# First layer: where the key searches of query blocks 4 to 7 run, and the order in which the blocks are attended

## What is computed

```python
logits = jnp.einsum('bqhd,bsd->bqhs', qi, k_idx)
score = jnp.einsum('bqh,bqhs->bqs', wi, jax.nn.relu(logits))
score = jnp.where(causal[None], score, -jnp.inf)
_, idx = lax.top_k(score, topk)            # topk = 256
c_sel = jax.vmap(lambda c, i: c[i])(c_kv, idx)
s = jnp.einsum('bqhr,bqkr->bhqk', qa, c_sel)
p = jax.nn.softmax(jnp.where(valid[:, None], s, -jnp.inf), axis=-1)
```

## Time and profile before

| | us |
|---|---|
| median of three runs | 4326.2 |
| span of the profiled execution | 4323.5 |
| second half of stage 1, last input tile turned to last projection | 457 to 800 |
| stage 2, recurrence and attention of layer one | 827 to 2172 |

### The profile page before, as it was taken

How to read it: one execution, slowest core, us unless ns; L and a number is a source line. 1 busy time by engine, 2 the same in 40 slices (tenths; PEclk the granted TensorE clock), 3 DMA queues, 4 the chain that set the end, 5 groups by cost and what they waited for, 6 DMA issues and landing times. The chain is left out here.

```text
span 4323.5 us, 76198 instructions
## 1 busy us (share of the span) xinstructions
PE 3949.5 (91%) x31096; PEld 2780.8 (64%) x31096; DVE 2669.1 (62%) x5092; ACT 2122.4 (49%) x3127; POOL 1204.6 (28%) x966
## 2 busy tenths in 40 slices
PE   7989999878988998888789899898999999999889
PEld 5767776546666666666477687686555555555567
DVE  5555555556777787788675323345677777777543
ACT  4444444397777888787443322222333333333431
POOL 1111111125344344434111000000444445454200
PEclk9999999887999999999789999999999999999999
DMA  3334233402111111211255544465232323231243
GB/s 124 95 115 131 83 99 102 124 20 50 34 42 39 47 44 37 56 44 48 86 181 186 197 138 147 167 217 175 52 77 54 80 61 77 55 81 34 99 141 107
DMA packets 388093, 404.95 MB, mean 94 GB/s; under 512 B 115776, under 2 KB 287488, under 8 KB 387488
## 3 DMA queue, kind: packets, MB, share of 16 engines
q1 hardware_dynamic: 386656, 396.77, 31.3%
q10 hardware_dynamic: 1088, 3.32, 0.2%
HBM read 248.36 MB, written 151.62 MB: 93 GB/s over the span
## 5 line engine op out<-in xcount | busy, mean ns | idle before, releaser
L142 ACT ACTIVATE PT<-psum 128x1024 f32<-128x1024 f32 x384 | 394.3, 1027 | 659.6 <-PE psum L132 659.1
L170 DVE TENSOR_REDUCE m<-psum 128x1 f32<-128x1024 f32 x384 | 467.9, 1221 | 274.8 <-PE psum L132 274.8
L132 PE MATMUL psum<-xc,wah 128*128 128x512 f32 x1600 | 514.8, 403 | 3.2 <-DVE xc L146 2.9
L146 POOL TENSOR_TENSOR part<-PT 128x1024 f32<-128x1024 f32 x144 | 341.5, 2371 | 471.4 <-DVE all L146 379.1
L132 PE MATMUL psum<-PT,V 128*64 128x512 f32 x1536 | 371.5, 605 | 0.0
L143 ACT ACTIVATE bias<-score,cand,cols 128x2048 bf16<-128x2048 f32 (+6 forms) x217 | 314.8, 1451 | 85.9 <-DVE cand L153 79.5
L146 POOL TENSOR_TENSOR Lm<-gm,cst 64x512 f32<-64x512 f32 x192 | 257.6, 1342 | 349.9 <-PE psum L132 194.2
L132 PEld LDWEIGHTS psum<-xc,wah 128*128 128x128 f32 x1600 | 300.0, 190 | 79.4 <-issue 10.3
L143 ACT ACTIVATE sgn<-score,cand,cols 128x1920 bf16<-128x1920 f32 (+6 forms) x217 | 291.4, 1343 | 89.5 <-DVE cand L153 84.8
L132 PE MATMUL psum<-hc,w4h 128*128 128x512 f32 x1024 | 320.3, 394 | 8.7 <-DVE w4l L146 8.7
L132 PE MATMUL psum<-xc,wal 128*128 128x512 f32 x800 | 315.9, 395 | 0.0
(11 more groups left out here) (336 smaller groups left out, 8664.9 us busy)
## 6 DMA issues: line engine op xcount, KB each, us to landing
raw_a<-in_w_a SPq DMA_DIRECT2D x50, 512.0 KB
raw_w<-in_w_in SPq DMA_DIRECT2D x32, 512.0 KB, 5.3
QNh<-scr_qnh SPq DMA_DIRECT2D x48, 256.0 KB, 4.9
QRh<-scr_qrh SPq DMA_DIRECT2D x96, 128.0 KB, 4.6
QNl<-scr_qnl SPq DMA_DIRECT2D x48, 256.0 KB, 6.4
xin<-in_x SPq DMA_DIRECT2D x16, 512.0 KB
scr_AR<-AR SPq DMA_DIRECT2D x32, 256.0 KB, 2.2
scr_BK<-BK SPq DMA_DIRECT2D x32, 256.0 KB, 2.2
```

The source lines that it names most:

```text
L132: return self.e.matmul(out, a, b, start=start, stop=stop, skip_group_check=True)
L142: return self.e.activation(out, src, f, bias=bias, scale=scale)
L146: return self.e.tensor_tensor(out, a, b, op) if self.e else self.vector(out)
L170: return self.e.tensor_reduce(out, a, AX, op, negate=negate) if self.e else self.vector(a)
```

## The change

The searches of blocks 7, 6, 5 and 4 move from stage 2 into stage 1, after the last input tile is turned. The search code becomes one set of functions (`index_pe`, `index_act`, `index_dve`, `index_pool`) that both stages call with their own buffers (class `Search`). In stage 1 the searches take freed buffers: the two input tiles for the scores, the scratch of the transposes for the keys and signs, and PSUM banks 4 and 5, which DVE reads directly after an in-place relu. Each finished bias is stored to DRAM, and stage 2 loads the four at its start. The blocks are then attended in the order 7, 6, 5, 4, 15, ..., 8, 3, 2, 1, 0; block 7 follows the keys and values in their round, blocks 6 to 4 have the next. The number of passes per search is the same.

```diff
+N_EARLY = 4
+BLOCKS = (7, 6, 5, 4, 15, 14, 13, 12, 11, 10, 9, 8, 3, 2, 1, 0)
...
+        early.score = xin
+        early.kidx, early.keys_there = [xtmp[1].rearrange("p a b -> p (a b)"), ekidx], (d_eki, 1)
+        signs = [xjunk, xtmp[0].bitcast(BF16).rearrange("p a b -> p (a b)")]
+        early.junk = early.out = lambda b: signs[early.lane(b)]
+        early.relu = lambda k, e: bank[4 + e]
+        order_e = []
+        for t in early.blocks + [N_EARLY]:
+            halves_e = ([index_half(t - 1, True)] if t else []) + ([index_half(t, False)] if t < N_EARLY else [])
+            order_e += weave(weight, *halves_e)
...
         order_a += carry_a
+        ready = order_a.index(("tr", NT - 1)) + 1
+        order_a = order_a[:ready] + merge(order_a[ready:], order_e)
...
+                elif k[0] == "qx":
+                    b = k[1]
+                    if early.no[b] == 0:
+                        q.wait_ge(n_act, "xh", NT - 1, 1)
+                        q.wait_ge(n_dve, "xl", NT - 1, 1)
+                        q.wait_ge(d_kv[1], 1)
+                        for c in range(2):
+                            q.dma(early.kidx[c][:, :], scratch["kidx"][:, 512 * c:512 * c + 512]).then_inc(*d_eki.up(c))
...
+                    q.dma(eqx[:, :, :], feat("q")[:, 4:6, 128 * nth(b):128 * nth(b) + 128]).then_inc(*d_eqx.up(b))
+                elif k[0] == "tie" and k[2] == last_of[k[1]]:
+                    b, n = k[1:]
+                    N = 128 * (nth(b) + 1)
+                    q.wait_ge(early.k_pool, "tie", b, n)
+                    q.dma(scratch["bias"][early.no[b]][:, 0:N], early.out(b)[:, 0:N]).then_inc(*d_ebo[early.lane(b)].up(b))
...
-        for t in range(-1, NT + 1):
-            parts = [attend_pieces((t - 1,))] if t > 0 else [kv_order] if t < 0 else []
-            parts += [index_half(t, True)] if 0 <= t < NT else []
+        first = late.blocks[0]
+        for t in range(first - 1, NT + 1):
+            if t < first:
+                parts = [kv_order + attend_pieces((0,))]
+            elif t == first:
+                parts = [attend_pieces(range(1, first))]
+            else:
+                parts = [attend_pieces((t - 1,))]
+            parts += [index_half(t, True)] if first <= t < NT else []
             parts += [index_half(t + 1, False)] if t + 1 < NT else []
...
         def sp_2(q):
+            for b in early.blocks:
+                N = 128 * (nth(b) + 1)
+                q.dma(bias_of(b)[:, 0:N], scratch["bias"][early.no[b]][:, 0:N]).then_inc(*d_eb.up(b))
             for k in q.pieces(turns_2):
```

More of the change, by code:

```diff
@@ new lines, in index_pieces @@
+        def index_pieces(b):
+            if nth(b) < TOPK // 128:
+                return [("nobias", b)]
+            ns = [n for n, _, _ in chunks(128 * (nth(b) + 1))]
+            out = [("qx", b)] + [("log", b, n, x) for n in ns for x in range(2)] + [("sel0", b)]
+            for i in range(30, -1, -1):
+                out += [("bit", b, i), ("flip", b, i)]
+            return out + [("selA", b), ("selB", b), ("selC", b), ("selD", b)] + [(x, b, n) for n in ns for x in ("eq", "sel2", "tie")]
@@ new lines, in program, with index_pe @@
+        early, late = Search("e", list(range(N_EARLY))), Search("l", [b for b in range(N_EARLY, NT) if nth(b) >= TOPK // 128])
+        INDEX = ("log", "sel0", "bit", "flip", "selA", "selB", "selC", "selD", "eq", "sel2", "tie")
+        def index_pe(q, I, k):
+            b, n, x = k[1:]
+            w = width(b, n)
+            m = I.no[b] % len(I.qx)
+            q.wait_ge(I.d_qx[m], b)
+            q.wait_ge(*I.keys_there)
+            for e in range(2):
+                o, free = I.ring[k][e]
+                if free:
+                    q.wait_ge(*free)
+                a = 64 * e
+                t = q.mm(o[:, 0:w], I.qx[m][a:a + 64, x, :], I.kidx[n][a:a + 64, 0:w])
+            t.then_inc(*I.x_pe.up("log", b, n, x))
@@ L570, in sp_a @@
                 q.wait_ge(d_kv[e], 3)
+            for e in range(2):
+                q.wait_ge(d_ebo[e], early.blocks[-2 + e])
             q.wait_ge(d_AR, len(subs) - 1)
@@ L668, in act_a @@
                 what = k[0]
+                if what in INDEX:
+                    index_act(q, early, k)
+                    continue
                 if what == "in":
@@ L947, in pool_a @@
                 what = k[0]
+                if what in ("log", "eq", "tie"):
+                    index_pool(q, early, k)
+                    continue
                 if what == "in":
@@ L1542, in act_2 @@
+                elif what in INDEX:
+                    index_act(q, late, k)
                 elif what == "exp":
@@ L1694, in dve_2 @@
+                elif what in INDEX:
+                    index_dve(q, late, k)
                 elif what == "score":
```

437 lines of the change are left out of this document (245 added, 192 removed).

## The result

The changed kernel took 4231.65 us (median, 4227.33 to 4233.34), beside 4324.94 for the kernel before on the same chip: ratio 0.9781, 95% interval 0.977 to 0.9793. I had forecast 4278. The direction was right, the gain of 93 us was nearly twice the 48 that the sum gave. All differences between a kernel and before are of medians on the same chip, and kernels of different chips are compared by their ratios; those of a stage are between two profiled executions. Ratios of different chips are themselves uncertain by about 0.2%: the changed kernel, taken again on another chip, came to 0.9801 instead of 0.9781, while its two stages ended at 2078.3 us instead of 2078.6, so that difference lies behind the stages that this document is about.

What follows compares the result with a forecast made beforehand. PE was taken to bound the second stage with some friction, except 134 us waiting for block 15's search. +17 + 12 + 2 - 79 = -48 against the 4323.5 us span: 4275.5, or 4278 as a run; range 4222 to 4345.

Steps and rivals of the forecast that it cites:

- step 2: Second stage, 832 to 2076 us: 1037 us of PE work at 89% takes 1165 instead of 1244, -79 us.
- the hole: Second stage, 900 to 1034 us: PE waits for block 15's search; attention of blocks 7 to 4 fills it.
- Its cover: Second stage: block 15's search ends about 1075, before attention of 7 to 4 ends near 1140; 65 us of cover.
- Step 1: First stage, 457 to 800 us: takes on four searches; logits +17, hold-ups +12, SP's issues +2 us.
- +12 for friction: First stage: PE at about 93% because copies and chains wait on ACT and DVE, +12 us (ends 0 and +56).
- The logits' +17: First stage: logits of the four blocks lie on PE's path, +17 us (ends 13.5 and 20.8).
- beyond 880 step 1 is wrong: Sign: the stage boundary (first kT matmul) moves from 827 to about 858; beyond 880 refutes the first-stage estimate.
- The friction rival: First stage: ACT can't be filled above 80.7%, +56 us; kernel still faster at 4305; chance 0.20.
- The +2 for SP's issues: Start of second stage: four bias loads stand in front of everything, 0.51 us per issue, +2 us.
- The 40 us of hidden drain: First stage: by the skill page, 32 table loads would hide an estimated 40 us more of ACT; not counted.
- Slower: Rival, first stage: ACT becomes its bound, deciding below 77% share; at 72% kernel +27, 4353 us; chance 0.15.
- More gain: Rival: PE at 92% in the second stage, first at its 96%; -98 us, 4228; chance 0.12.

Runs made afterwards that it cites:

- the thin matmuls: Kernel before, with the logits' matmuls of blocks 4 to 7 in stage 2 computing 64 columns instead of up to 512: 4336.03 us, ratio 1.0015.
- the buffer mended: Changed kernel with three early searches (7, 6, 5) instead of four, and block 15 given the free bias tile: 4206.44 us, ratio 0.9727.
- The first form with three early blocks: Changed kernel with three early searches (7, 6, 5), block 15's bit passes writing into the tile holding biases of 7 and 6: 4270.2 us, ratio 0.9857.
- the placing by weight: Changed kernel, early searches woven in by estimated costs of pieces instead of their count: 4225.11 us, ratio 0.9768; repeated on another occasion 4229.0, 0.977.
- the form without ranking: Changed kernel whose four early searches leave out the ranking of ties, a bias of zeros being stored: 4213.21 us, ratio 0.9749.
- logits alone: Changed kernel with only the logits of the four early searches left in stage 1, no bit steps or ranking: 4206.67 us, ratio 0.9722.
- logits with ranking and two steps: Changed kernel whose four early searches take 2 steps instead of 31, all else kept: 4195.29 us, ratio 0.9708.

## Why the prediction was right in sign and wrong in size

**What failed is step 2**, in its sentence "I don't go above 89% although 170 us of ACT and 90 of DVE have left". It held the stage to be PE's work over a share. The runs show another stage. Of the -146.3 us, 88.3 come from the removal of the searches, and the columns of the logits on PE, which my sum took as the only work that leaves, gave none of it by themselves: with 14.4 us less in that group the stage was 6.4 longer. The gain came with ACT's bit passes (43.6), the ranking over POOL and DVE (20.9) and the logits' relus and accumulations (20.6 beyond the thin matmuls). The 88.3 and the 57 of the order are measured; this split is less sure, as each form has an order of its own. Many of PE's short waits, which I saw spread over the stage and took as given, were waits for answers from the engines that I relieved: those for Y alone fell from 44.2 to 12.2 us. In numbers of my sum, over the same stretch (it began 5 us into the stage, here at 887): PE is busy 996.2 us instead of 1037 (-46 at my 89%), at 90.4% (-17), and the tail is 92 instead of 96. So two thirds of the miss stand under PE's busy time and not under its share. But that busy time is no independent term: it fell by 17 and by 27 us when nothing but bits or ranking left, with every matmul still there. The sum was wrong in its form, fixed work over a fixed share, and not only in one size. Two sizes were too small beside it: the logits' group 32.2 measured against 17, and the stretch 32 to 37 over the whole stage against 20 from the one window; they overlap, as said.

**The order**, 57 us, was in the prediction: the hole goes, and the first masked score comes within 70 us. Its cover held, but with 9 us and not the 65 that I had: the last piece of block 15's bias ends at 1143.45, where I had 1075, and its first score stands at 1152.45, where I had 1140. With three early blocks and the buffer mended there is no slack left; the score waits for POOL again, though only for 0.56 us of DVE's time (the changed kernel, then that form):

```profile
1141.52 1.93 POOL L155 TENSOR_SCALAR bias<-rl 128x512 bf16<-128x512 f32 x1
...
1152.45 0.68 DVE L180 CUSTOM_DVE_ANT_0 P<-psum,bias 128x512 f32<-128x512 f32 x1
```
```profile
1095.92 0.69 DVE L180 CUSTOM_DVE_ANT_0 P<-psum,bias 128x512 f32<-128x512 f32 x1 [0.56 <-POOL bias L155]
```

Of this cover I wrote that "without it each us of delay is a us of stage". The first form with three early blocks tried that: its bits began 116 us later than with the buffer mended (1011.9 against 895.8), block 15's first score 92 us later (1188.1 against 1095.9), and the stage took 61 us more, so two thirds of the score's delay.

**Step 1** was undersized in the term of +12 for friction. The logits' +17 was 15.8 by busy time. The rest of 55 is 39, and by my own mark ("beyond 880 step 1 is wrong") it was wrong, by 2 us. My argument that the planner's price of a bit pass keeps ACT on time looked at the length of a pass, not at what stands together with it, and its comparison was wrong: the price of 1.29 us includes the read of the sum, and with it a pass takes 1.32. That is 4 us in 124 passes and explains little. The size is no constant of the stage: the placing by weight takes 12 us of it, and three searches cost 20.4 in all, so that the fourth, a fifth of the columns, costs 34.6. The friction rival had stage 1 right (+56, ACT at 80.7%; it showed 79.5) and the rest wrong. The +2 for SP's issues does not show: without the early searches, but with their loads and stores of biases, stage 2 starts at 827.29 instead of 827.24. No table load was added (33 against 35). The 40 us of hidden drain were put on loads that both kernels have, so they could not have changed the difference between them.

**The rivals.** Slower was priced on ACT under 77% in the first stage; up to the last projection it was at 78.6, 1.6 points away. More gain named nearly the right time, 4228, by luck: its first stage at 96% did not happen and cost 36 us more than it had, and its second gave 29 us more, so the two errors cancel. My own sum had the same luck in part, 24 us too little cost against 67 too little gain. More gain rested on PE not being at a ceiling. The row of 1152 to 1989 has PEld at 548.7 of 837 us, 65.6% against 63% before, beside PE at 89.9%, and the thin matmuls left PE with 14 us less work and no shorter stage. Neither looks like a bound at 89%. The Trainium skill, "Perfetto Trace Analysis", section "Identifying the Most-Contended Engine", says that matmul busy time doesn't tell how near PE is to its limit and judges PE's headroom by the share of weight loads and the floating-point work done. The trace agrees in that the share of weight loads left room and the thin matmuls won nothing; a much higher matmul share was not reached, 90.4% against 89.3%.

**What stays open.** Why thin matmuls made the kernel slower by 0.15%, and why logits alone cost stage 1 more than logits with ranking and two steps, was not followed up; the order planned anew would explain both, but no form kept the order and changed one part, which is the test that is missing. The 64 matmuls of the logits, as against their columns, were never removed alone. That the ranking beside the reciprocals makes the first hole fits the form without ranking; the second hole outlives the ranking, and its cause is open. The placing experiments moved more than that one meeting.

## What to carry to other kernels

An engine that is 89% busy in many short waits is not the bound because its share is the highest: ask whose answers it waits for. Taking work off those engines can be worth more than taking it off the busiest one; here 122 us of short ACT passes were worth 44 us of the stage, and 14 us of PE nothing, each in an order planned anew. Where a planner makes the order, hold the order fixed when you take a part out, or the form measures two changes. Do not divide a fixed busy time by a fixed share: both moved when the waits did. Search work put beside a stage that is full costs by where its pieces meet other chains; try the number of moved pieces (here three, not four) and where each buffer's former user ends before weighing costs. Read a buffer's rotation anew whenever the order changes: one tile that came free late cost 61 us here, order included.

## What the runs showed of the hardware that I had not expected

The granted clock makes a hole cost more than its own length. In the form with the late search, stage 2 had 167.4 us at 1.2 GHz, with the buffer mended 96.0; from 457 to the start of stage 2 the changed kernel had 83.6, the kernel before 35.7. In the two places of the changed kernel the clock fell to 1.2 GHz at 610.8 and at 689.3; PE had been busy 2.1 of the 5.5 us before the one and 5.4 of the 9.0 us before the other. The 48 matmuls of raw with w_uq took 603 ns on average in the kernel before, none of them at 1.2 GHz. In the changed kernel the 29 at 2.4 GHz took 606 ns and the 19 at 1.2 GHz 1080.

On DVE, the ranking's 512-wide scan took 1.21 us once and 1.74 the next time (this one starts from a carried sum), and its product 0.74 and 1.85 us for the same shape. POOL was idle during the first scan and product, and had this work during the second:

```profile
615.72 1.12 POOL L163 COPY Pc<-PP 128x4 f32<-128x4 f32 x1
616.80 1.46 POOL L148 TENSOR_TENSOR dd<-pb 128x768 f32<-128x768 f32 x1
```

Whether the one slows the other was not tried.
